# State-space recurrence of one mixer: from 16 tiles of 256 steps to chunks of four tokens over all tiles

## What is computed

```python
mag = exp(lr * dt); ab_re, ab_im = mag * cos(li * dt), mag * sin(li * dt)
bu_re = einsum('bsgp,gnp->bsgn', uf, bb_re)      # 16 channels of a group -> 64 states
bu_im = einsum('bsgp,gnp->bsgn', uf, bb_im)
# x[t] = a * x[t-1] + bu[t], complex, for all 256 steps t
_, _, x_re, x_im = associative_scan(combine, (a_re, a_im, bu_re, bu_im), axis=1)
y = einsum('bsgn,gpn->bsgp', x_re, c_re) - einsum('bsgn,gpn->bsgp', x_im, c_im)
y = gelu(y + d_skip * u)
y = y * sigmoid(y @ glu_w + glu_b)
```

## Time and profile before

| | us |
|---|---|
| median of three runs (1232.1 to 1239.67) | 1234.69 |
| the profiled execution | 1239.51 |
| its span in the profile | 1237.5 |
| PE busy | 1155.0 (93%) |
| DVE busy | 801.6 (65%) |
| ACT busy | 562.0 (45%) |
| POOL busy | 258.6 (21%) |

### The profile page before, as it was taken

The page is one execution under the profiler, slowest core; times in us unless marked ns, Lnnn a source line. Parts: engine busy times, 40 slices in busy tenths (PEclk is TensorE's granted clock), DMA queues, the critical chain, the costliest instruction groups (busy, mean ns, idle before and its releaser), DMA issues.

```text
span 1237.5 us, 20184 instructions
## 1 busy us (share of the span) xinstructions
PE 1155.0 (93%) x7906; PEld 1047.6 (85%) x7906; DVE 801.6 (65%) x1109; ACT 562.0 (45%) x757; POOL 258.6 (21%) x195
## 2 busy tenths in 40 slices
PE   6999998889989999989859999999899689999997
PEld 6999998785689999989858999999776369999996
DVE  4766667655468988666744766666767645766665
ACT  6544345444565445565464544344311146434433
POOL 0500000230039999000100100000288800000000
PEclk9999998996999999999889999999898899999999
DMA  8645544340045555443322655545221203544540
GB/s 298 258 171 202 177 179 153 105 168 34 1 166 193 205 194 196 179 168 120 124 99 102 224 188 199 188 169 203 103 68 69 95 8 141 217 184 172 203 166 38
DMA packets 34460, 189.56 MB, mean 153 GB/s; under 512 B 3824, under 2 KB 4592, under 8 KB 18032
## 3 DMA queue, kind: packets, MB, share of 16 engines
q1 hardware_dynamic: 31968, 181.42, 40.0%
q10 hardware_dynamic: 2160, 6.50, 1.5%
q0 software_dynamic: 288, 1.05, 0.2%
HBM read 187.90 MB, written 1.05 MB: 153 GB/s over the span
## 4 chain that ended last, share of the span: by engine, by line
PE 79%; POOL 7%; DVE 5%; ACT 5%; issue 3%; DMA 1%; ACTq 0%; SPq 0%; DVEq 0%; POOLq 0%
PE ps L458 40%; PE ps L471 19%; PE ps L508 8%; PE ps L525 5%; POOL scratch L1703 4%; PE ps L543 2%; PE ps L567 2%; POOL chw L1690 1%; POOL chw L1692 1%; ACT gu_high L756 1%; DVE gu_low L1124 1%; PE ps L556 1%; DMA gu_raw<-in_wgu 1%; ACT hT_high L793 1%; PE ps L420 1%
## 5 line engine op out<-in xcount | busy, mean ns | idle before, releaser
L458 PE MATMUL ps<-hT_high,gu_high 128*128 128x256 f32 x1408 | 399.4, 284 | 5.2 <-DVE hT_low L1158 5.2
L458 PE MATMUL ps<-hT_low,gu_high 128*128 128x256 f32 x1408 | 399.1, 283 | 0.0
L458 PE MATMUL ps<-hT_high,gu_low 128*128 128x256 f32 x1408 | 399.1, 283 | 0.0
L458 PEld LDWEIGHTS ps<-hT_high,gu_high 128*128 128x128 f32 x1408 | 270.6, 192 | 9.7 <-issue 4.0
L458 PEld LDWEIGHTS ps<-hT_low,gu_high 128*128 128x128 f32 x1408 | 270.6, 192 | 3.1
L458 PEld LDWEIGHTS ps<-hT_high,gu_low 128*128 128x128 f32 x1408 | 270.7, 192 | 0.0
L818 ACT ACTIVATE gu_high<-gu_raw 128x2048 fp32r<-128x2048 f32 x86 | 164.7, 1915 | 127.4 <-PE ps L458 127.3
L1209 DVE TENSOR_TENSOR gu_low<-gu_raw,gu_high 128x2048 fp32r<-128x2048 f32 x86 | 199.9, 2324 | 20.2 <-ACT gu_high L818 20.1
L756 ACT ACTIVATE gu_high<-gu_raw 128x2048 fp32r<-128x2048 f32 x40 | 76.7, 1916 | 170.8 <-PE ps L508 131.3
L1193 DVE TENSOR_TENSOR ffn_s<-scratch,ps 128x256 f32<-128x256 f32 x88 | 36.8, 418 | 164.2 <-PE ps L458 164.2
L1124 DVE TENSOR_TENSOR gu_low<-gu_raw,gu_high 128x2048 fp32r<-128x2048 f32 x40 | 94.7, 2368 | 74.5 <-ACT gu_high L756 74.4
(11 more groups left out here) (214 smaller groups left out, 1925.7 us busy)
## 6 DMA issues: line engine op xcount, KB each, us to landing
gu_raw<-in_wgu SPq DMA_DIRECT2D x126, 1024.0 KB, 4.8
dn_raw<-in_wdn SPq DMA_DIRECT2D x88, 512.0 KB, 5.2
x<-in_x SPq DMA_DIRECT2D x2, 512.0 KB, 5.1
gu_raw<-in_wgu SPq DMA_DIRECT2D x2, 512.0 KB, 6.8
scratch<-in_glu ACTq DMA_DIRECT2D x1, 1024.0 KB, 6.9
chw<-in_biasM ACTq DMA_DIRECT2D x1, 1024.0 KB, 4.8
out_x<-scratch SPq DMA_DIRECT2D x4, 256.0 KB, 2.4
s5in<-in_s5in ACTq DMA_DIRECT2D x1, 768.0 KB, 6.9
```

The lines of the kernel that those rows point to most:

```text
L458: i = nc.tensor.matmul(bank(4 + 2 * w + h)[:, 0:SEQ], gu[pw_][:, sl, o:o + P], hT[px][:, k, :], start=(pw_, px, k) == (0, 0, 0), stop=(pw_ ...
```

## The change

The recurrence now runs over 64 chunks of four tokens. `uT` is kept with the place in the chunk outside and the chunk inside, 4 x 64 columns. PE makes what a chunk adds to the state at its end, with the input weights times powers 0 to 3 of the transition (`bb(k, part)`), 128 products of 64 columns (L719 of the new kernel). One scan of the real and one of the imaginary part then cover all 16 tiles, 16 x 64 = 1024 steps in four rows of four tiles, with the magnitude to the fourth power; `mag_row` holds it, with a 0 where a tile begins. What lies within a chunk goes past the state: `lag` holds, for distances of 0 to 3 tokens, the product of output weights, power and input weights (8 transposes on L693, 64 small products on L706), and 64 products on L732 apply it to `uT`. 128 products of 63 columns (L740) add the state of the chunk before, through output weights times powers 1 to 4 (`cc`). All banks 4 to 7 hold the chunk inputs at once. The projections stand between: two before `lag` is made, one after it, five between L719 and L732.

On DVE the multiplications are four of 128 x 1024 (L1571) in place of 32 of 128 x 512, the two scans have 1024 steps each (L1563), and the three-step rotations back are on DVE as well (L1560, L1585, L1590). POOL has one difference left in the mixer; ahead of it POOL has a quarter of the angle tables, the four powers of `bb` (L1745), and in the third feed-forward 48 multiplications and sums for `cc` and the four copies of `mag_row`. ACT copies the transposed weights and `lag` out of PSUM behind its first two splits, and takes 2 passes of table sines in place of 8.

```diff
 TWO_PI = 2 * math.pi
+S5_T = 4
...
-        zz, dC, dS = (take(2 * 512).rearrange("p (r h s) -> p r h s", r=2, h=2) for _ in range(3))
+        s5P1, s5P4, mag_row = (take(1024).rearrange("p (q c) -> p q c", q=4) for _ in range(3))
+        s5P2, s5P3 = chw[:, 0:4, :], chw[:, 4:8, :]
...
+            pe.wait_ge(s["bb_ready"], 4 * S5_T)
+            for part in range(2):
+                for c in range(4):
+                    i = nc.tensor.transpose(bank(4 + part)[:, c * P:(c + 1) * P], bb(0, part)[:, c, :], ident[:, :])
+            i.then_inc(s["bT_psum"], 1)
             project(2, 1, 5, True)
+            pe.wait_ge(s["cc_ready"], 1)
+            pe.wait_ge(s["bT_ready"], 1)
+            for c in range(4):
+                for first in (True, False):
+                    for part in range(2):
+                        for q in range(4):
+                            j = 4 * c + q
+                            rhs = (c_raw[:, part, j, :] if first
+                                   else cc(part, j // 8)[:, j % 8, 0:S5_T - 1, :].rearrange("p k m -> p (k m)"))
+                            a0 = c * P + (0 if first else 32)
+                            i = nc.tensor.matmul(bank(6)[32 * q:32 * q + 32, a0:a0 + (32 if first else 96)],
+                                                 b_state[:, part, c, 32 * q:32 * q + 32], rhs,
+                                                 start=part == 0, stop=part == 1)
+            i.then_inc(s["lag_psum"], 1)
+            project(2, 2, 5, True)
             wait_unit(pe, 2, 1)
-            pe.wait_ge(s["bb_ready"], 4)
-
-            def s5_in(j):
-
-                c, q = j // 4, j % 4
-                if j >= 2:
-                    pe.wait_ge(s["s5_mod"], 2 * (j - 1))
-                r0 = slice(32 * q, 32 * q + 32)
+            pe.wait_ge(s["lag_ready"], 1)
+            pe.wait_ge(s["rB_ready"], 5)
+            for c in range(4):
                 for part in range(2):
-                    i = nc.tensor.matmul(bank(4 + j % 2)[:, part * SEQ:(part + 1) * SEQ],
-                                         bb[r0, part, c, :, :].rearrange("p g n -> p (g n)"),
-                                         uT[r0, c, :], start=True, stop=True)
-                i.then_inc(s["bu_done"], 1)
-
-            def s5_out(j):
-
-                c, q = j // 4, j % 4
-                pe.wait_ge(s["s5_dem"], 2 * (j + 1))
-                out = bank(6, 2)[32 * q:32 * q + 32, c * SEQ:(c + 1) * SEQ]
-                r = j % 2
-                terms = [(0, dC[:, r, 0, :]), (2, dS[:, r, 1, :]), (1, dS[:, r, 0, :]), (1, dC[:, r, 1, :])]
-                for k, (w, z) in enumerate(terms):
-                    i = nc.tensor.matmul(out, cc[:, w, j, :], z, start=k == 0, stop=k == 3)
+                    for b in range(S5_T):
+                        for q in range(4):
+                            r0 = slice(32 * q, 32 * q + 32)
+                            i = nc.tensor.matmul(
+                                bank(4 + q)[:, part * SEQ + c * S5_C:part * SEQ + (c + 1) * S5_C],
+                                bb(S5_T - 1 - b, part)[r0, c, :], uT[r0, c, b * S5_C:(b + 1) * S5_C],
+                                start=b == 0, stop=b == S5_T - 1)
+            i.then_inc(s["bu_done"], 1)
+            for v in range(3, 8):
+                project(2, v, 5, v < 6)
+            pe.wait_ge(s["s5_mod"], 4)
+            for c in range(4):
+                out = bank(6 + c // 2)[:, c % 2 * SEQ:(c % 2 + 1) * SEQ]
+                for l in range(S5_T):
+                    for q in range(4):
+                        r0 = slice(32 * q, 32 * q + 32)
+                        nc.tensor.matmul(out[r0, l * S5_C:SEQ], lag[r0, c, l, :], uT[r0, c, 0:SEQ - l * S5_C],
+                                         start=l == 0, stop=False)
+                if c == 0:
+                    pe.wait_ge(s["s5_dem"], 2)
+                for b in range(S5_T):
+                    for part, X in ((0, s5P4), (1, s5P1)):
+                        for q in range(4):
+                            j = 4 * c + q
+                            i = nc.tensor.matmul(
+                                out[32 * q:32 * q + 32, b * S5_C + 1:(b + 1) * S5_C],
+                                cc(part, j // 8)[:, j % 8, b, :], X[:, q, c * S5_C:(c + 1) * S5_C - 1],
+                                start=False, stop=(b, part) == (S5_T - 1, 1))
                 i.then_inc(s["y_done"], 1)
...
+                    nc.scalar.activation(chw[:, 4:8, :], bank(4, 2), ACT.Copy).then_inc(s["bT_ready"], 1)
+                if v == 1:
+                    act.wait_ge(s["lag_psum"], 1)
+                    nc.scalar.activation(lag.rearrange("p c l m -> p (c l m)"), bank(6), ACT.Copy) \
+                      .then_inc(s["lag_ready"], 1)
+            act.wait_ge(s["s5_dem"], 2)
             act.dma_start(biasM, a["biasM"]).then_inc(s["biasM_loaded"], 16)
             for c in range(4):
                 act.wait_ge(s["y_sum"], c + 1)
@@ -1095,7 +1145,8 @@
...
-            dve.wait_ge(s["y_done"], S5_TILES)
+                    i = nc.vector.tensor_tensor(in_time(uT[:, 2 * v + h, :]),
+                                                bank(v % 4)[:, h * SEQ:(h + 1) * SEQ].rearrange("p (s b) -> p s b", b=S5_T),
+                                                rB.rearrange("p (s b) -> p s b", b=S5_T), ALU.mult)
+                i.then_inc(s["vfree"], 1)
+                gu_low(MIX_ITEM[2] + v + 2)
+            evacuate(2, 2, qM[:, 0:2, :])
+
+            def v_of(part):
+
+            def scan(out, src):
+                step.mark(nc.vector.tensor_tensor_scan(
+                    out.rearrange("p q c -> p (q c)"), mag_row.rearrange("p q c -> p (q c)"),
+                    src.rearrange("p q c -> p (q c)"), 0.0, ALU.mult, ALU.add))
+
+            dve.wait_ge(s["trig"], 2)
+            dve.wait_ge(s["cc_ready"], 1)
+            dve.wait_ge(s["bu_done"], 1)
+            for out, part, tab in ((s5P3, 1, tabC), (s5P4, 0, tabS), (s5P1, 0, tabC), (s5P2, 1, tabS)):
+                nc.vector.tensor_tensor(out, v_of(part), tab, ALU.mult).then_inc(s["s5_mod"], 1)
+            evacuate(2, 3, qM[:, 2:4, :])
+            dve.wait_ge(s["s5_mod"], 4)
+            product(s5P1, s5P1, s5P2, ALU.add)
+            step.done(dve)
+            scan(s5P2, s5P1)
+            evacuate(2, 4, kM[:, 0:2, :])
+            dve.wait_ge(s["s5_sub"], 1)
+            step.done(dve)
+            scan(s5P1, s5P3)
+            product(s5P4, s5P2, tabC)
+            step.done(dve)
+            product(s5P3, s5P1, tabS)
+            step.done(dve)
+            nc.vector.tensor_tensor(s5P4, s5P4, s5P3, ALU.subtract).then_inc(s["s5_dem"], 1)
+            evacuate(2, 5, kM[:, 2:4, :])
+            product(s5P1, s5P1, tabC)
+            product(s5P2, s5P2, tabS)
+            step.done(dve)
+            nc.vector.tensor_tensor(s5P1, s5P1, s5P2, ALU.add).then_inc(s["s5_dem"], 1)
...
-                reduce_angle(ang, k, t, (C1, C2))
-                nc.gpsimd.tensor_scalar(ang, ang, 3.1415925, -3.1415925, ALU.min, ALU.max) \
-                  .then_inc(s["angles"], 1)
-
-            pool.wait_ge(s["s5_trig"], 4)
+            for j in range(S5_TILES):
+                step.mark(nc.gpsimd.tensor_scalar(tabS[:, j % 4, j // 4 * S5_C:(j // 4 + 1) * S5_C],
+                                                  trow[:, 0:SEQ:S5_T], s5s["th"][:, j:j + 1], None, ALU.mult))
+            step.done(pool)
...
+            for k in range(S5_T):
+                if k:
+                    tt(A[4], A[0], cs, ALU.mult)
+                    tt(A[5], A[1], sn, ALU.mult)
+                    tt(A[6], A[0], sn, ALU.mult)
+                    tt(A[7], A[1], cs, ALU.mult)
+                    pool.wait_ge(s["bb_ready"], 4 * k)
+                    tt(A[0], A[4], A[5], ALU.subtract)
+                    tt(A[1], A[6], A[7], ALU.add)
+                for part in range(2):
+                    for g in range(2):
+                        nc.gpsimd.tensor_scalar(bb(k, part)[:, :, g * HD:(g + 1) * HD],
+                                                A[part].rearrange("p (c n) -> p c n", n=HD),
+                                                col(COL_SEL + g), None, ALU.mult).then_inc(s["bb_ready"], 1)
...
+            tt(L[0][0], s5s["mag"], s5p["cos"], ALU.mult)
+            tt(L[0][1], s5s["mag"], s5p["sin"], ALU.mult)
+            complex_product(L[1], L[0], L[0])
+            complex_product(L[2], L[1], L[0])
+            complex_product(L[3], L[1], L[1])
+            tt(w2, s5s["mag"], s5s["mag"], ALU.mult)
+            tt(s5s["dt"], w2, w2, ALU.mult)
...
+            for q in range(4):
+                step.mark(nc.gpsimd.tensor_copy(
+                    mag_row[:, q, :].rearrange("p (c n) -> p c n", c=4),
+                    s5s["dt"][:, q:S5_TILES:4].unsqueeze(2).broadcast_to([P, 4, S5_C])))
+            step.done(pool)
+            step.mark(nc.gpsimd.memset(mag_row[:, :, 0:SEQ:S5_C], 0.0))
+            ts(c_im, c_im, -1.0, None, ALU.mult, ALU.bypass)
```

(56 more changed lines are left out.)

133 lines of the change are left out of this document (40 added, 93 removed).

## The result

The changed kernel takes 1186.91 us in the median of 4 runs (1183.87 to 1189.60), against 1233.39 (1231.90 to 1239.67) for the one before on the same chip: a ratio of 0.961, with a 95% interval of 0.957 to 0.966. It is faster by 46.5 us, about twice the 23.6 that were forecast, and the time lies just under the lower end of the range (1187), near where the first rival ("four abreast", 1189) had put it. The profiled execution took 1188.6.

What follows compares the result with a forecast made beforehand. POOL was taken to bound the tile loop. PE's terms from 884.25 us summed to an end at 967.7 instead of 991.25, a gain of 23.6: 1215.9 for the profiled execution, 1211 against the median; range 1187 to 1250.

Steps and rivals of the forecast that it cites:

- the first rival: Short PE products run four abreast on four array parts: 22.3 instead of 44.8 us, time 1189; chance 0.22.
- What bounds the kernel before: Tile loop, 884.25 to 991.25 us: its chain belongs to POOL; perfect overlap could give back 31 us.
- POOL ahead of the mixer at no cost: Second and third feed-forwards: POOL's coefficient work is covered by PE, costed at nothing, with over 100 us of room.
- I take this pace, two abreast and never under 0.055: PE's L706, L719, L732, L740: 7.0, 14.1, 9.6 and 14.1 us, together 44.8 against 41.5 before.
- My low bound of 22.3 us: PE's four kinds of short products if four run abreast: half of 44.8 us.
- The high bound: PE's four kinds one after another at 0.11 us: 14.1 + 28.2 + 18.6 + 28.2 = 89 us.
- The sum: PE from the second projection's end, 884.25, to the end of L740: ends at 967.7 instead of 991.25.
- That page's caution against cutting small dimensions: Skill page cited against the change on PE: take no tiling factor from an already small dimension; estimate left at 44.8 us.
- DVE's side: DVE chain behind chunk inputs: 17.4 us, scans 2.2 each, last split 1.6 late, state ready 11 before L740.
- Behind it nothing changes: After L740: skip term, gelu, gate and attention keep their order, with 11 and 13 us as before.

Runs made afterwards that it cites:

- one quarter at a time: Changed kernel with the q loop outermost in all four short-instruction groups, so queue neighbours use the same array quarter: 1239.33 us, ratio 1.002.
- with two: Changed kernel with the same loops in pairs, only q and q+1 as neighbours and the other two quarters behind them: 1202.88 us.

## Why the prediction was wrong in size

- *What bounds the kernel before*: right. The loop over tiles belonged to POOL, and that loop is gone. But this alone brought nothing: with one quarter at a time and POOL just as idle the time is 1239.
- *POOL ahead of the mixer at no cost*: right. The feed-forwards took 188.0 and 187.8 us, and nothing waits for a coefficient.
- *"I take this pace, two abreast and never under 0.055"*: this step failed, for the number of parts abreast and for the floor. Measured per instruction: `lag` 0.015 (2.0 us for 7.0), chunk inputs 0.029 (7.3 for 14.1), within the chunk 0.038 (4.9 for 9.6), state 0.018 (4.6 for 14.1). Four run abreast, and the floor of 0.055, read from a pair of 128-column products in the earlier trace rows, was no floor but those columns' price: with 63 columns two abreast take 0.027. My low bound of 22.3 us, half of the estimate, kept the floor in it; the measured sum is 18.7. (The high bound has 18.6 for the part within the chunk where twice 9.6 is 19.2; nothing hangs on it.) With four abreast in the sum the stretch would have come out right to 1 us, partly by luck. The sum had 83.4 us for it, 82.1 without the 1.3 for the transposes, which stand ahead of the second projection; 82.1 - 44.8 + 22.3 = 59.6, and 58.7 were measured, but the 3.6 us too many for the short instructions nearly cancel against the 2.9 us of gaps that the sum did not have.
- The Trainium skill, "TensorEngine Tiling (Array Packing)", Performance Considerations, has about 60 cycles as the least price of a product, an estimated 0.025 us. The trace does not agree for four abreast: 0.016 for a state instruction of 63 columns. That page's caution against cutting small dimensions did not bite either. The changes of mode between L732 (32 rows) and L740 (128 rows) do cost something, but little: in the records the first L732 instruction starts 0.168 us after the start of the last group of L740, where two groups of L740 are 0.055 apart. With all of L732 ahead of the last projection the two kinds took 4.48 + 3.54 + 0.45 = 8.5 us without their gap instead of 4.88 + 4.56 = 9.4, so the changes came to about 1 us. The Trainium skill's factor of 3.07 for four row tiles of 512 columns ("TensorE: Matmul & The Clock Gate", Part 3) is nearer the mark than two abreast, but not what the trace shows for short ones. The row tiles here, products that lie on different rows of the array, are the chunk inputs, with 0.112 us for one alone and 0.112 for a group of four, so 4.0; the state groups, which lie on different columns, have the same 4.0 at 0.055, and their 3.07 / 1.02 = 3.0 has the packed seams and the changes of mode in it. That case was a rival with 0.22; it should have been the forecast.
- *DVE's side*: right. Scans 2.29 us (2.2), the wait for the last split 1.9 (1.6), the state ready before PE asks, by 3.7 us rather than 11, since PE came earlier.
- *Behind it nothing changes*: off by 2.6 us. 1.7 of them are the gate at half clock (8.85 us for 7.16), 0.7 the split L1605, which now puts y back into the order of time and reads it with a stride (2.09 for 1.42).
- *Not foreseen*: 2.9 us of standing still for instructions.

## What to carry to other kernels

Where products have 32 rows or 32 weight columns, put the ones for different parts of the array next to each other in the queue: this order was worth some 50 us of 1239 here, without one instruction less (about 12 of them were the half clock in the chunk inputs). Price a group of neighbours by its slowest member (weight columns or moved columns), not each product by a floor, and ask then whether the instructions come fast enough: a burst of some 250 pairs at 0.016 us ran dry. When a single time is no better than 5 us, compare the stretch between two instructions of the same trace.

## What the runs showed of the hardware beyond that

- The clock fell in the chunk inputs when their order was unpacked. PE was 100% busy in them in all three orders; four abreast the grant stayed at 1.00, with one quarter 37.8 us of the loop ran at 0.50, with two 15.7 us. There the unpacked order paid twice. It is no rule for one quarter, though: in the same run with one quarter at a time L732 and L740 also ran without a pause, and from 971.8 to 991.7 us the grant was 1.00. What makes the difference was not tried.
- With one quarter at a time `lag` took 0.023 us per instruction, under half of the 0.056 expected. It has only eight instructions per quarter, so much of it lies at the seams between two quarters; whether that is all of it is not shown.
- PE's instruction supply: gaps of 0.2 to 3.3 us, 256 instructions apart where there are two, and gone in two of the three versions that have the gate's slower products between. Why the next block isn't asked for sooner is open.
